# A two-block fp32 network on one core: raw and split weight slots re-divided, the first products in another order, unread products and constants moved

## The reference

```python
def first_block(x, p, positions, ...):
    h = rms_norm(x, attn_norm_w)
    x = x + hybrid_mixer(h, ...)      # SSD scan beside attention, 7440 input columns
    h = rms_norm(x, moe_norm_w)
    x = x + hier_moe(h, ...)          # 4 groups of 8 experts, 256 wide each
    gate = sigmoid(rms_norm(x, ple_norm_w) @ w_ple_gate)
    x = x + gate * (p @ w_ple)
    return rms_norm(x, final_norm_w)

def second_block(x, ...):
    h = rms_norm_2(x, g_norm)         # one projection: Hyena input, q/kv, gates
    u = short_conv(hy_in, ...)        # two long convolutions, in frequency space
    ...                               # beside it attention with low-rank q and kv
    return x + (g_hy * u_hy + g_at * u_attn) @ w_out
```

## Time and profile before

| what | us |
|---|---|
| median of three runs | 813.55 |
| the three runs | 812.01, 813.55, 817.29 |
| the profiled execution | 816.31 |
| its span in the trace | 814.5 |

### The profile page before, as it was taken

One profiled execution on the slowest core, in us unless ns is written; L12 is line 12 of the kernel. 1 busy time (PEld: TensorE's weight loads), 2 busy tenths in 40 slices (PEclk: granted clock), 3 DMA queues, 4 the chain that ended last, 5 costly groups with the idle time before them and its releaser, 6 DMA issues.

```text
span 814.5 us, 11000 instructions
## 1 busy us (share of the span) xinstructions
PE 739.3 (91%) x4606; PEld 558.0 (69%) x4606; DVE 466.3 (57%) x825; ACT 323.4 (40%) x479; POOL 17.8 (2%) x14
## 2 busy tenths in 40 slices
PE   4999999989999998976798798689999989799998
PEld 4978886878877885553344354348999856578886
DVE  5778965545766656432252131048687788845673
ACT  5554446536536425210111010046755514255631
POOL 0000000000000000000000000001100003000000
PEclk9999999999999999996899898899999999989999
DMA  9656543133538859699999999996373744333311
GB/s 319 185 208 206 193 138 133 57 104 102 155 120 325 315 237 423 278 377 420 423 419 420 421 420 422 410 355 222 116 237 94 247 154 151 108 104 104 103 52 52
DMA packets 62578, 189.98 MB, mean 233 GB/s; under 512 B 7417, under 2 KB 11771, under 8 KB 50044
## 3 DMA queue, kind: packets, MB, share of 16 engines
q1 hardware_dynamic: 60750, 184.44, 60.9%
q10 hardware_dynamic: 1774, 4.79, 1.7%
HBM read 188.17 MB, written 1.05 MB: 232 GB/s over the span
## 4 chain that ended last, share of the span: by engine, by line
PE 62%; DVE 14%; DMA 12%; ACT 8%; issue 3%; POOL 0%; SPq 0%; ACTq 0%; DVEq 0%
PE pb L519 58%; DMA raw<-in_w_exp_up 7%; DVE WL L1755 4%; PE pb L528 4%; ACT WH L1256 3%; DMA WHo<-in_w_exp_up 2%; DMA WLo<-in_w_exp_down 1%; ACT arena L1415 1%; DMA raw<-in_w_in 1%; DVE cv_ L1862 1%; DVE arena L2021 1%; DVE arena L1808 1%; ACT arena L1284 1%; POOL small L2649 0%; DVE arena L2067 0%
## 5 line engine op out<-in xcount | busy, mean ns | idle before, releaser
L1755 DVE TENSOR_TENSOR WL<-raw,WH 128x2048 fp32r<-128x2048 f32 (+5 forms) x80 | 173.4, 2178 | 87.4 <-ACT WH L1256 87.3
L1256 ACT ACTIVATE WH<-raw 128x2048 fp32r<-128x2048 f32 (+5 forms) x80 | 144.9, 1822 | 80.7 <-PE pb L519 71.2
L519 PE MATMUL pb<-WH,HTh 128*128 128x512 f32 (+2 forms) x384 | 156.2, 407 | 6.0 <-ACT arena L1284 3.1
L519 PE MATMUL pb<-WL,HTh 128*128 128x512 f32 (+2 forms) x384 | 148.8, 387 | 0.0
L519 PE MATMUL pb<-WH,HTl 128*128 128x512 f32 (+2 forms) x384 | 148.5, 387 | 0.0
L519 PEld LDWEIGHTS pb<-WH,HTh 128*128 128x128 f32 x384 | 73.0, 190 | 24.9 <-issue 5.1
L519 PEld LDWEIGHTS pb<-WL,HTh 128*128 128x128 f32 x384 | 72.8, 190 | 14.6
L519 PEld LDWEIGHTS pb<-WH,HTl 128*128 128x128 f32 x384 | 73.1, 190 | 13.3 <-issue 1.0
L519 PE MATMUL pb<-arena 128*32 128x256 f32 (+6 forms) x252 | 59.3, 435 | 12.2 <-issue 8.8
L519 PE MATMUL pb<-WH,arenao 128*128 128x512 f32 x192 | 59.6, 392 | 1.2 <-DVE arenao L1789 1.2
L2296 DVE TENSOR_TENSOR rt_<-rt_,pb 128x256 f32<-128x256 f32 x8 | 3.4, 421 | 87.6 <-ACT rt_ L1531 87.6
(11 more groups left out here) (366 smaller groups left out, 1264.5 us busy)
## 6 DMA issues: line engine op xcount, KB each, us to landing
raw<-in_w_in SPq DMA_DIRECT2D x46, 1024.0 KB, 5.2
raw<-in_w_exp_up SPq DMA_DIRECT2D x18, 1024.0 KB, 20.2
arena<-in_w_exp_down SPq DMA_DIRECT2D x14, 1024.0 KB, 12.8
arena<-in_w_exp_gate SPq DMA_DIRECT2D x13, 1024.0 KB, 22.7
raw<-in_w_out SPq DMA_DIRECT2D x8, 1024.0 KB, 5.2
WHo<-in_w_exp_down SPq DMA_DIRECT2D x8, 1024.0 KB, 18.0
WLo<-in_w_exp_down SPq DMA_DIRECT2D x8, 1024.0 KB, 20.5
raw<-in_w_exp_gate SPq DMA_DIRECT2D x7, 1024.0 KB, 12.1
```

What stands on the lines that cost most here:

```text
L519: return e.matmul(o, l, r, start=start, stop=stop, skip_group_check=True)
L1256: e.activation(h_, r_, ACT.Copy).then_inc(hi.sem, hi.mark(k))
L1755: e.tensor_tensor(l_, r_, h_.bitcast(F32), ALU.subtract).then_inc(lo.sem, lo.mark(k))
```

## The change

- `NRAW` is 6 and `NSPLIT` is 4. WL is gone: DVE writes the low part over the raw weight in its slot (named `rawo` where it is read as fp32r). The total of slots stays ten. `fetch(k)` waits for PE's last product with tile k - 6. The split runs one tile further ahead. The buffers of the experts are the same memory in another list.
- `channels_by_part` runs the first channel tile term by term: for four chunks all high by high, all low by high, all high by low, and the same for the other four.
- 28 products of the identity with itself, which nobody reads, stand ahead of the first transposes.
- ACT asks for `cst1` behind the squares of the first norm. The -0.5 is set by a memset on POOL.
- A second `keep_warm` stands behind the rank.
- The down products of the first round take the banks of the last two gathered pieces, the gate products those of the first two.
- Layer 0 of the filter and the transposition of p move from the end of round 1 into round 2, ahead of its gathers, on PE, DVE and ACT.
- After the experts `weights(None, dense_again + 3)` stands in place of `weights(dense_again)`.

A 2048-wide low part stands ahead of the first copy in place of a 1024-wide one. The diff, cut to its core:

```diff
-NRAW = 4
-NSPLIT = 3
+NRAW = 6
+NSPLIT = 4
...
-        shared = (("WH", [128, NSPLIT, SLOT], F32R), ("WL", [128, NSPLIT, SLOT], F32R), ("HDh", [128, 1280], F32R),
+        shared = (("WH", [128, NSPLIT, SLOT], F32R), ("raw", [128, NRAW, SLOT], F32), ("HDh", [128, 1280], F32R),
...
+            def channels_by_part(key, names, ready, drainers, within):
+                o = [ring.take(name, by) for name, by in zip(names, drainers)]
+                for c0 in (0, 4):
+                    k = chunk_at[key][c0][0]
+                    w = tile_parts(k)
+                    for l, r in ((0, 0), (1, 0), (0, 1)):
+                        (hi, lo)[l].wait_ge(e, k)
+                        for c in range(c0, c0 + 4):
+                            if r:
+                                ve.wait_ge(e, (ready, c))
+                            else:
+                                ac.wait_ge(e, (ready, "hi", c // 2 * 2))
+                            for i, name in enumerate(names):
+                                ins = mul(o[i][:, 0:256], w[l][:, c - c0, 128 * i:128 * i + 128], HT[r][:, c, :],
+                                          c == 0 and l == r == 0, c == 7 and r == 1)
...
             d_c0.wait_ge(e, "in")
+            for i in range(28):
+                mul(banks[7][:, 0:128], ident, ident)
             rows_T("n1")
...
-            channels(("cx", 0), [("xbc", g) for g in range(4)], 512, "n1", [ve] * 4, columns_T)
+            channels_by_part(("cx", 0), [("xbc", g) for g in range(4)], "n1", [ve] * 4, columns_T)
...
             keep_warm()
+            keep_warm()
...
-            yb = [ring.of[(ring.i + i) % 4] for i in range(2)]
-            ring.of, ring.i = [ring.of[(ring.i + i) % 4] for i in (2, 3)], 0
+            yb = [where[("xg", 0, j)] for j in (2, 3)]
+            ring.of, ring.i = [where[("xg", 0, j)] for j in (0, 1)], 0
...
+                if q == 2:
+                    d_c2.wait_ge(e, "in")
+                    d_filt.wait_ge(e, "in")
+                    filter_layer(0, f1[:, :], C["zT"][0:33, :])
+                    side_input_T()
                 for j in gathers(q):
                     gather(q // 2 + 1, j)
...
-                if q == 1:
-                    d_c2.wait_ge(e, "in")
-                    d_filt.wait_ge(e, "in")
-                    filter_layer(0, f1[:, :], C["zT"][0:33, :])
-                    side_input_T()
...
-            e.dma_start(c1[:, 128:], A["cst1"]).then_inc(d_c1.sem, d_c1.mark("in", by=16))
...
             norm_rows("n1", X)
+            e.dma_start(c1[:, 128:], A["cst1"]).then_inc(d_c1.sem, d_c1.mark("in", by=16))
...
-            weights(dense_again)
+            weights(None, dense_again + 3)
...
-            mh = C["mhalf"]
+            e.memset(mh, -0.5).then_inc(po.sem, po.mark("mh"))
+            po.wait_ge(e, "mh")
...
-            d_c1.wait_ge(e, "in")
...
                 elif k >= NRAW:
-                    lo.wait_ge(e, k - NRAW)
+                    mm.wait_ge(e, ("tile", k - NRAW))
```

More of the change, by code:

```diff
@@ L53, in constants @@
     one["ones"] = np.ones((128, 4))
-    one["mhalf"] = np.full((128, 4), -0.5)
     two = {}
@@ L259, in program @@
         hs8 = [sm(2, 8), sm(2, 8)]
[L260 removed]
+        mh, mh8, nhq = sm(4), sm(2, 8), sm(2, 8)
         wr = sb("wr", [128, 8, 36])
@@ L459, in tile_parts @@
             c, n = tiles[k]["shape"]
-            return tuple(x[:, tiles[k]["slot"], 0:c * n].rearrange("p (c n) -> p c n", c=c) for x in (WH, WL))
+            return tuple(x[:, 0:c * n].rearrange("p (c n) -> p c n", c=c)
+                         for x in (WH[:, tiles[k]["slot"], :], raw_r[:, k % NRAW, :]))
         def tile_flat(k):
@@ L555, in fill @@
                     gemm_chunk(name, key, c, open_fill[name], lhs, ready, turned)
+            def channels_by_part(key, names, ready, drainers, within):
[13 more added lines that the diff above has]
+                                          c == 0 and l == r == 0, c == 7 and r == 1)
+                                if c == 7 and r == 1:
+                                    ins.then_inc(mm.sem, mm.mark(name, *([("tile", k)] if i == len(names) - 1 else [])))
+                        if c0 == 4 and l == r == 0:
+                            within()
+                    if c0 == 0:
+                        ins.then_inc(mm.sem, mm.mark(("tile", k)))
             def channels(key, names, n, ready, drainers, within=None):
@@ L1253, in weights @@
                     elif k >= dense_again:
-                        i = held_split + 2 * emptied.index(tiles[k]["slot"])
-                        mm.wait_ge(e, held_last[i][0:2], held_last[i + 1][0:2])
+                        mm.wait_ge(e, held_last[held_high[k - dense_again]][0:2])
                     e.activation(h_, r_, ACT.Copy).then_inc(hi.sem, hi.mark(k))
@@ L1524, in spectrum, with filter_sine @@
                     ac.sem, ac.mark(("ks", c - 1)))
+            def filter_sine(n):
+                ve.wait_ge(e, ("fh", n))
+                e.activation(FH[:, 1, :], FH[:, 0, :], ACT.Sin).then_inc(ac.sem, ac.mark(("fh", n)))
             for q in range(8):
@@ L1531, in scalar @@
                 e.activation(HG[q % 2], pb(("gu", q))[:, 0:256], ACT.Silu).then_inc(ac.sem, ac.mark(("su", q)))
+                if q == 2:
+                    filter_sine(0)
+                    mm.wait_ge(e, "pT")
+                    e.activation(PT_, pb("pT")[:, :].rearrange("p (c l) -> p c l", c=2), ACT.Copy).then_inc(
+                        ac.sem, ac.mark("pT"))
                 for j in gathers(q):
@@ L2693, in fetch_held @@
                     ve.wait_ge(e, ("mg", 1))
[L2694 to L2697 removed]
+                elif i < 19:
+                    mm.wait_ge(e, ("tile", emptied[i - 9][0]))
                 else:
@@ L2706, in sync @@
                 e.dma_start(X[:, t, :], xr[:, t, :]).then_inc(d_x.sem, d_x.mark("in", by=16))
-            for k in range(NRAW):
+            for k in range(4):
                 fetch(k)
@@ L2723, in sync @@
                 e.dma_start(dst, bc(A[n])).then_inc(d_early.sem, d_early.mark("in", by=16))
-            for k in range(NRAW, 6):
+            for k in range(4, 6):
                 fetch(k)
```

54 lines of the change are left out of this document (23 added, 31 removed).

## The result

The changed kernel takes 819.24 us, the median of 17 runs (813.61 to 823.52), the kernel before 813.63 (17 runs, 812.01 to 817.65). The ratio is 1.006 with a 95% interval of 1.0043 to 1.0077: slower by 3.5 to 6.3 us. It also spreads over 10 us, where the kernel before spreads over 5.6. The profiled execution took 818.64 us, its span is 816.8, so it is 2.3 longer than the profiled one of before: less than the medians' 5.6. Both the loss and that gap have to be explained.

A forecast was written before the change was run, and what follows sets the result against it. PE, busy 739.3 of 814.5 us, was taken as the bound, with expert-weight DMA bounding 366 to 530. Terms 0.0 - 1.1 + 1.8 + 0.85 - 1.6 - 0.6 + 0 = -0.65 gave a median of 812.9, range 809.0 to 816.6.

The forecast's parts named there:

- Six raw slots, one tile further ahead: Dense parts: splits one tile earlier give -1.1 at 52 us, +1.8 at the gated sum, +0.85 near 646; later raw release zero.
- asked for later: Near 52 us: DVE's depthwise taps move back by a split (2.3 us), but their banks are needed later than that.
- which the change does not touch: PE's larger pauses, beyond those at 52, 325, 331, 564 and 646 us, were taken as unaffected.
- the longer pauses at 562 and 646: Behind the experts: low parts ahead of the gated sum cost +1.8, and a later 384-wide copy +0.85.
- the pause at 325: Routing: a second unread product fills PE's 1.24 us pause and keeps the clock, -1.6 at two chances in three.
- The unread products: Head: 28 products from 4.8 to 12.25 us take over the slow stretch; first product at 14.4, value taken as 0.
- Routing: Ahead of the experts: clock kept -1.6 and bank order -0.6, together -2.2, reaching the end of the kernel.
- the bank pause: At 331.29 us: PE's 0.61 us pause for the last copy out of the gather banks goes, -0.6.
- Filter: Within the experts: PE's 8.78 us pause ahead of 371.16 goes or shrinks, worth zero, at best -1.
- Constants and memset: Head: later cst1 request and memset of -0.5 are worth zero, at most 0.5 either side.
- The rivals: Clock not kept, 814.5 (0.26); held raw slots, 823.3 (0.06); experts bound by PE, 804.1 (0.06); unread products slow, 816.6 (0.12).
- held raw slots: Near 643 us: slots held until the last product make two loads late, +10.4, giving 823.3; chance 0.06.

The follow-up runs named there:

- r_place: Changed kernel with its memory, but every split at its old place in the engines' programs: 808.39 us, ratio 0.9932.
- s_wait3: r_place, but ACT waits for the tile three back before writing a high part, though a fourth slot is there: 812.96 us, ratio 0.9995.
- p_routing: Kernel before with only the second keep-warm product and the bank order of the first expert products: 812.76 us, ratio 0.9985.
- r_best: r_place with 16 unread products in place of 28: 808.24 us, ratio 0.9926.
- t_best3: Changed kernel with splits at their old places except tile 7, one place earlier, and 16 unread products: 805.24 us, ratio 0.9897.
- s_place0: r_place without unread products: 806.98 us, ratio 0.9927.
- r_0: Changed kernel without unread products: 818.22 us, ratio 1.0044.

## Why the prediction was wrong

The forecast was 812.9 us with a range to 816.6; it came to 819.24. Of the 6.3 us between them, by the ledger and the estimate above, 2.8 are pauses that I did not see (1.6, 0.7 and 0.5), about 2.0 are falls of the clock behind new pauses, 0.9 are the unread products, and about 1.0 is the routing, whose gain I took in full.

- **Six raw slots, one tile further ahead: this step failed.** It counted -1.1 at 52 us, where the ledger has -1.4, and +1.8 and +0.85 behind the experts, which came as +1.7 and +1.1. It missed three other losses and one gain. The taps being "asked for later" was right, but ahead of them on DVE stands the copy L1897, whose bank PE asks for at 27 us: +1.6. Near 108 it missed +0.7, at the second half of the gated sum +0.5. The gain: it took the pause of 2.60 at 655, which both kernels have, as one "which the change does not touch", though the change brought the slot that removes it and spent it in the same edit: 4.6 us between r_place and s_wait3.
- **Terms without the clock: not sized.** I priced the longer pauses at 562 and 646 by their length alone. In three of five profiles each had a fall of 1.7 us behind. I had the rule for it in hand, for the pause at 325, and used it only for a gain.
- **The unread products: the mechanism right, the size off.** I had 9 products in 3.65 us at the low rate (0.40 each), then 0.20 each, done at 12.25. Measured: 12 products in 5.1 us at the low rate, done at 13.58, and XN came at 9.84. So +0.9 instead of 0. Windows of the changed kernel show the step, in the count of PE's records (two for each product). A count holds the records that reach in from outside too, so the rate is the rise from a short window to a longer one: 14 in 3 us, then 18 in 2 us, which is 0.43 and 0.22 us for a product. The prices were nearly right, the length of the slow stretch was not. The granted clock reads 1.00 throughout; here the count shows the pace and the column doesn't.

```profile
5.00:6.00 1.00, 1.00 (x5) 1.00 (x6) 0.00 (x0) 0.00 (x0) 0.00 (x0) 1.00 1.03 388
5.00:9.00 4.00, 4.00 (x19) 4.00 (x20) 1.98 (x4) 1.43 (x3) 0.70 (x1) 1.00 1.05 395
10.00:11.00 1.00, 1.00 (x11) 1.00 (x10) 0.34 (x1) 0.63 (x1) 0.00 (x0) 1.00 1.04 393
10.00:13.00 3.00, 3.00 (x29) 3.00 (x28) 2.29 (x1) 0.63 (x1) 0.00 (x0) 1.00 1.04 387
```

- **Routing: right in the trace.** -2.2 forecast, -1.9 seen: the clock stays up (1.3 of the 1.6 counted), the bank pause goes, and the stream follows. In time it is less (-1.2 in p_routing), which fits a fall that comes in only 3 of 6 profiles. By the Trainium skill (TensorE: Matmul & The Clock Gate, section "HAM oscillation — how this bites in real kernels") the clock goes down over waits much longer than these. The traces disagree: behind pauses of 1.24 and 1.75 us it fell in six of eleven profiles. Weighing the row above the rule was right.
- **Filter: right**, -0.7 with 0 in its interval. **Constants and memset**: timed only as part of the head. XN is ready at 9.84 in place of 10.39, 0.55 earlier where I had at most 0.5, and the 28 unread products hide it.
- **The base.** I carried a difference worked out on one execution over to the median. That execution held a fall at 537 us which the sum could not know; the error in the forecast is that of the terms, since only a difference was carried over.
- **The rivals.** None was it. The nearest, held raw slots, named the right edit and the wrong mechanism: in no profile is a pause of PE put down to the load of a dense tile. The chance of 0.06 for a loss by this edit was too small, given that the text itself had found two places where a split moved ahead of something PE waits for; two found by sampling meant that there were more.

## What to carry to other kernels

A deeper buffer and an earlier producer are two edits. Try the buffer with the program order left as it was: here the fourth high-part slot was worth 4.6 us (r_place against s_wait3), and running further ahead in the same instruction stream took 11, because early splits stood ahead of small copies for which the critical engine waited and used up the free slot. The deeper buffer with nothing else of the change was not run. When a producer's instructions move one place ahead in an engine's program, list every copy that they pass, over the whole program, and who waits for it. And price a new pause of TensorE with the chance of a clock fall behind it, not by its length.

## What the runs showed of the hardware

- The granted clock's falls behind equal pauses come in some executions and not in others (the table above): 0 of 14 behind 0.39 us, 0 of 9 behind 0.75, 9 of 11 behind 2.60. One fall costs up to 1.7 us here. The kernels with fewer such pauses were also steadier: 1 to 4.4 us of spread against 6 to 10, though in fewer runs.
- In the first microseconds PE ran at about half pace while the granted clock read 1.00. How long that lasted differed: to about 9 us in r_best, to 10 in the changed kernel, to 11 in t_best3, all with unread products from 4.8 to 5.0 on. Where PE began with the transposes at 10.0, it lasted to 13.8 in s_place0 and to 16.0 in r_0.
- Filling a pause with an unread product costs nothing where the pause is there anyway: the second keep-warm product took 0.85 us of a pause of 1.24 and did not delay the gather (from the end of cv_o to its first product it is 0.15 us with and without).
